# Attention begun after two token groups, gates and pools woven into its steps, pool chains cut into pieces

## What is computed

```python
z = h @ w_in[i]                                   # (B,S,3072)
q, k, v, g_attn, u, g_pool = ...                  # six slices of 512 columns each
lam = exp(sum(lam_q1*lam_k1)) - exp(sum(lam_q2*lam_k2)) + lam_init
# 4 heads, each with two 64-wide halves of q and k, and a 128-wide v; causal
o = (softmax(q1 k1^T / 8) - lam * softmax(q2 k2^T / 8)) v
attn_out = rms_norm(o, subln_g) * (1 - lam_init) * silu(g_attn)
# group g of 4: trailing mean over 2, 4, 8, 16 tokens, minus the token, then a 128x128 map
pool_out = ((mean_w(u) - u) @ w_pool) * pool_scale * silu(g_pool)
mix = concat([attn_out, pool_out]) @ w_out
h = layer_norm(2**0.25 * h + mix, ln_g, ln_b)
h = h + (p @ w_pe) * sigmoid(h @ w_pg + b_pg)
```

## Time and profile before

| | |
|---|---|
| device time, median of 3 (range) | 635.16 us (634.19 to 635.40) |
| profiled execution: device time, span | 635.05 us, 633.5 us |
| PE matmul busy | 598.1 us, 94% of the span |
| DVE busy | 383.1 us, 60% |
| ACT busy | 358.2 us, 57% |
| POOL busy | 158.5 us, 25% |
| mean granted PE clock, cores | 0.985 to 0.993 |

### The profile page before, as it was taken

The page is one execution under the profiler, slowest core; times in us unless marked ns, Lnnn a source line. Parts: engine busy times, 40 slices in busy tenths (PEclk is TensorE's granted clock), DMA queues, the critical chain, the costliest instruction groups (busy, mean ns, idle before and its releaser), DMA issues.

```text
span 633.5 us, 12632 instructions; the slowest of 8 cores (627.6 to 633.5 us)
## 1 busy us (share of the span) xinstructions
PE 598.1 (94%) x5282; PEld 331.5 (52%) x5282; DVE 383.1 (60%) x735; ACT 358.2 (57%) x520; POOL 158.5 (25%) x212
## 2 busy tenths in 40 slices
PE   6897999999999999999999999899999999999895
PEld 2343444446566554566666654455655566665442
DVE  2226833725767788344534664677876686687696
ACT  3210231348777774677788756376666566776132
POOL 0477530001111120101010110323333333333242
PEclk9999999999999999999999999899999999999899
DMA  8999904022040000401144199001211211131003
GB/s 234 319 304 298 264 9 67 0 34 34 2 68 1 2 3 1 67 1 33 37 70 67 34 134 223 10 2 67 69 67 67 68 68 67 67 135 67 34 34 133
DMA packets 28393, 51.64 MB, mean 82 GB/s; under 512 B 3248, under 2 KB 12848, under 8 KB 28336
## 3 DMA queue, kind: packets, MB, share of 16 engines
q1 hardware_dynamic: 18656, 40.61, 20.3%
q0 software_dynamic: 9680, 10.22, 10.8%
HBM read 52.66 MB, written 8.39 MB: 96 GB/s over the span
## 4 chain that ended last, share of the span: by engine, by line
PE 76%; DVE 10%; SPq 5%; DMA 3%; issue 2%; ACT 2%; POOL 1%; DVEq 0%; ACTq 0%
PE psum_all L541 29%; PE psum_all L852 17%; PE psum_all L819 10%; PE psum_all L682 8%; PE psum_all L749 7%; SPq L154 5%; PE psum_all L775 2%; DMA sb_kT<-w_in 2%; DVE sb_PT L835 1%; DMA sb_kT<-xT 1%; PE psum_all L727 1%; DVE sb_st L687 1%; DVE sb_arena L608 1%; ACT sb_PT L825 1%; POOL sb_mv L693 1%
## 5 line engine op out<-in xcount | busy, mean ns | idle before, releaser
L825 ACT ACTIVATE sb_PT<-psum_all 128x1024 bf16<-128x1024 f32 (+1 forms) x288 | 265.3, 973 | 113.0 <-PE psum_all L819 111.8
L541 PE MATMUL psum_all<-sb_xb,sb_wsec 128*128 128x512 bf16 x640 | 164.5, 386 | 11.2 <-ACT sb_wsec L429 5.2
L852 PE MATMUL psum_all<-sb_Vt,sb_PT 128*128 128x129 bf16 x2176 | 148.0, 221 | 4.6 <-DVE sb_PT L835 3.7
L852 PEld LDWEIGHTS psum_all<-sb_Vt,sb_PT 128*128 128x128 bf16 x2176 | 134.5, 98 | 33.6 <-DVE sb_PT L835 5.9
L541 PEld LDWEIGHTS psum_all<-sb_xb,sb_wsec 128*128 128x128 bf16 x640 | 57.1, 99 | 79.5 <-issue 18.9
L541 PE MATMUL psum_all<-sb_wsec,sb_xb 128*128 128x512 bf16 x384 | 94.2, 380 | 2.9 <-DVE sb_arena L596 1.3
L819 PE MATMUL psum_all<-sb_qT,sb_kT 64*128 64x256 bf16 (+1 forms) x1152 | 87.0, 267 | 1.9 <-DVE sb_mixT L633 1.5
L819 PEld LDWEIGHTS psum_all<-sb_qT,sb_kT 64*128 64x128 bf16 x1152 | 44.5, 94 | 67.0 <-ACT sb_PT L825 30.3
L682 PE MATMUL psum_all<-sb_wsec,sb_mixT 128*128 128x512 bf16 x256 | 64.0, 386 | 0.4 <-DVE sb_mixT L905 0.4
L749 PE MATMUL psum_all<-sb_wsec,sb_arena 128*128 128x512 bf16 x224 | 57.1, 384 | 4.1 <-DVE sb_arena L737 2.5
L886 POOL TENSOR_TENSOR sb_sm<-sb_sm,sb_sc 128x2 f32<-128x2 f32 x32 | 7.6, 239 | 211.8 <-ACT sb_qT L884 116.8
(11 more groups left out here) (137 smaller groups left out, 583.4 us busy)
## 6 DMA issues: line engine op xcount, KB each, us to landing
sb_Vt<-w_in SPq DMA_DIRECT2D x28, 256.0 KB, 9.9
sb_kT<-w_in SPq DMA_DIRECT2D x20, 256.0 KB, 10.0
sb_Vt<-xT SPq DMA_DIRECT2D x16, 256.0 KB, 12.3
sb_kT<-xT SPq DMA_DIRECT2D x16, 256.0 KB, 12.0
sb_xb<-xT POOLq DMA_DIRECT2D x4, 1024.0 KB, 9.9
sb_xb<-x_own SPq DMA_DIRECT2D x7, 512.0 KB, 3.5
out<-sb_xb SPq DMA_DIRECT2D x7, 512.0 KB, 2.6
sb_wsec<-w_out POOLq DMA_DIRECT2D x2, 1024.0 KB, 10.4
```

The lines of the kernel that those rows point to most:

```text
L541: P.op(PE, lambda e: e.matmul(ps[:, bank, :], a, b, start=(kc == 0), stop=(kc == 7)), reads=[B_w[sec], wk[kc], bx, xk[kc]], writes=[B_bank ...
L825: P.op(ACT, lambda e, u=u, pi=pi, q0=q0: e.activation(out=PT[pi][:, :, :, q0:256].rearrange("p k c n -> p c k n"), in_=ps[:, 2 * u:2 * u + ...
L852: P.op(PE, lambda e, u=u, k=k, s=s, kb=kb, qb=qb, c=c, pi=pi, fresh=fresh, done=done: e.matmul(ps[:, BO + qb, c * 130:c * 130 + 129], PT[p ...
```

## The change

Attention starts when groups 0 and 1 are done (k, v, and q, gate and pool of group 1). The steps of j = 1 no longer alternate with those of j = 0. There are four fills in place of three: `fill0` under j = 0 (k2, v2, k3, v3, q3), `fill1` under j = 1 and `fill2` under j = 2 (`woven` for groups 3 and 5, then k, v, q of the next own group), and `fill3` under j = 3 (gates and pool of group 7, then the output part of 13 tiles; tile 13's first product goes behind the last step). Both blocks are gone. SiLU becomes a tanh on ACT and a multiplication on DVE that both read the bank (`twice_silu`), with the factor one half moved into two constants. Pool chains go out in pieces, two at each tick (two ticks to a step); a chain still pending is flushed at the next `q_u` or `q_y`. `take` goes on behind a finished quantum when 0.6 us or more of its share is left. Temporaries move to parts of `mixT` and `qT`, and the order of the first loads changes: w_in's q columns come before the third x group, small constants before the halo.

```diff
         while t < us and self._open():
             d, done = self._one()
             t += d
-            if done:
+            if done and us - t < 0.6:
                 break
...
+        for kc in range(8):
+            round_(POOL, wsec[0][:, kc, :], fetch(w_src(0, kc)), B_wk[0][kc])
...
         def more_loads():
-            for kc in range(8):
-                round_(POOL, xb[0][:, kc, :], fetch(x_src(2, kc)), B_xk[0][kc])
+            for dst, srcd in ((hl[:], hl_d), (gscb[:], sublng_d.rearrange("d o -> o d").partition_broadcast(128)),
+                              (lamv[:], lamv_d.partition_broadcast(128))):
+                P.dma(SP, dst, srcd, dsc)
+            P.dma(SP, cnt[:], cnt_d, dsc3)
+            P.dma(SP, pscale[:], pscale_d, dsc3)
+            P.dma(POOL, tri3[:].rearrange("p c n -> p (c n)"), tri_d, dsc2)
+            P.dma(POOL, ident[:], ident_d, dsc2)
+            P.dma(POOL, wpool[:], wpool_d.rearrange("(g c) d -> c g d", c=128), dsm)
...
+            for s_ in (4, 3, 5):
+                for kc in range(8):
+                    round_(POOL, wsec[s_][:, kc, :], fetch(w_src(s_, kc)), B_wk[s_][kc])
...
         def tick():
             now[0] += 1
+            for _ in range(min(2, len(chain))):
+                chain.popleft()()
             for f in ticks.pop(now[0], []):
                 f()
...
+        def twice_silu(bank, i, out_ap, view, writes):
+            src = ps[:, bank, :].rearrange("p (a n) -> p a n", a=2)
+            P.op(ACT, lambda e: e.activation(out=gt[i][:], in_=src, func=AF.Tanh, scale=0.5), reads=[B_bank[bank]], writes=[B_gt[i]])
+            P.op(DVE, lambda e: e.scalar_tensor_tensor(out=out_ap, in0=view(gt[i][:]), scalar=1.0, in1=view(src), op0=ALU.add, op1=ALU.mult),
+                 reads=[B_gt[i], B_bank[bank]], writes=writes)
...
+            chain.extend(parts + [difference])
...
-            order += [(0, 0, h), (1, 1, h), (0, 1, h), (1, 0, h)]
-        order += [(j, hf, h) for j in (2, 3) for hf in range(2) for h in range(4)]
+            order += [(0, 0, h), (0, 1, h)]
+        order += [(j, hf, h) for j in (1, 2, 3) for hf in range(2) for h in range(4)]
...
+        side_by_side(q_v(1), range(4, 8))
+        lam_ops()
+        side_by_side(q_q(1), range(4))
+        a, o, u, g, y = parts_of(1)
+        run_all(o + u[:2] + [a[0], u[2], a[1], a[2], u[3], a[3], g[0], g[1], y[0], g[2], y[1], g[3], y[2], hook(y[3], third_own)],
+                [4, 5, 6, 7, 0, 1, 2, 3])
...
+        def woven(s, k, v, f):
+            a, o, u, g, y = parts_of(s)
+            return [a[0], k[0], a[1], k[1], a[2], k[2], a[3], k[3]] + o + [u[0], v[0], u[1], g[0], u[2], g[1], y[0], u[3],
+                                                                         g[2], y[1], g[3], y[2], hook(y[3], f)] + v[1:]
+
+        fill0 = q_k(2) + hooked(q_v(2), lambda: load_xb(4)) + q_k(3) + q_v(3) + q_q(3)
+        fill1 = woven(3, q_k(4), hooked(q_v(4), lambda: load_xb(6)), lambda: load_xb(5)) + q_k(5) + q_v(5) + q_q(5)
+        fill2 = woven(5, q_k(6), hooked(q_v(6), load_p), lambda: load_xb(7)) + q_k(7) + hooked(q_v(7), load_wout) + q_q(7)
...
+        own7 = o + [a[0], u[0], a[1], u[1], a[2], u[2], hook(a[3], out_1), hook(u[3], load_wpg)]
+        own7 += [g[0], g[1], y[0], g[2], y[1], hook(g[3], out_2), y[2], hook(y[3], out_3)]
+        fill3 = own7 + fillD
...
-        for f in both_halves(q_G, 15, 1, 0):
+        for f, f2 in zip(both_halves(q_G, 15, 1, 0), p15):
             f()
-        for f in p15:
-            f()
+            f2()
```

More of the change, by code:

```diff
@@ L369, in build_nc @@
         B_PT = [Buf() for _ in range(4)]
-        B_g = B_PT[0:2]
+        B_gt, B_psc = [Buf() for _ in range(6)], Buf()
         B_o12 = [Buf() for _ in range(6)]
-        B_rr = [Buf() for _ in range(6)]
         B_sm = [Buf() for _ in range(6)]
@@ L591, in q_halo, with go_on @@
             return [Quantum([mm(p, kc) for p in range(4) for kc in range(8)], end, 32 * 0.03)]
+        def go_on(n):
+            for _ in range(min(n, len(chain))):
+                chain.popleft()()
         def pool_chain(p, j, bank):
+            go_on(9)
             w = POOL_W[p]
@@ L990, in build_nc, with out_1, out_2, out_3 @@
                 fillD += [q_T(k)]
-        def block(s):
-            ga, gp, y = q_ga(s), q_gp(s), q_y(s)
-            run_all(ga + [gp[0], gp[1], y[0], gp[2], y[1], gp[3], y[2], y[3]], [6, 7, 0, 1, 2, 3])
-            P.op(ACT, lambda e: e.activation(out=sc[:, 8:9], in_=sc[:, 0:1], func=AF.Exp), reads=[B_sc], writes=[B_sc])
-        def start_out():
+        def out_1():
+            olds = list(B_w[3].w.values()) + list(B_w[3].r.values())
+            wload(wpe[:], wpe_d.rearrange("(kc p) n -> p kc n", p=128), [B_w[3]])
+            after(8, lambda: P.op(DVE, lambda e: e.tensor_scalar(out=wpe[:], in0=wpe[:], scalar1=0.5, scalar2=None, op0=ALU.mult),
+                                  reads=[B_w[3]], writes=[B_w[3]]))
+            P.dma(SP, lngb[:].rearrange("p a n -> p (a n)"), lng_d.partition_broadcast(128), dsv, deps=olds)
+        def out_2():
+            olds = list(B_w[5].w.values()) + list(B_w[5].r.values())
+            for dst, srcd in ((lnbb, lnb_d), (bpgb, bpg_d)):
+                P.dma(SP, dst[:].rearrange("p a n -> p (a n)"), srcd.partition_broadcast(128), dsv, deps=olds)
+            t_vec.append((dsv.sem, dsv.cnt))
+        def out_3():
             for i in (1, 2):
@@ L1092, in build_nc @@
         last = steps[NS - 1]
-        M = {(t, nh): q_M(t, nh) for t in (14, 15) for nh in range(2)}
+        M = {(t, nh): q_M(t, nh) for t in (13, 14, 15) for nh in range(2)}
         av(NS - 1)
-        finish_one()
+        feed.drain()
         for p in sorted(fins):
@@ L1102, in build_nc @@
         tail[0] = True
+        for b in B_z15:
+            inherit(b, [B_gz[3]])
         norm, q_last = q_end(last)
@@ L1105, in build_nc @@
         run("fin_o", "fin_a")
-        for q, b in rest:
-            q.end(b)
-        rest.clear()
-        stats_of(("st", 13, 0))
-        finish_one()
-        assert not feed._open()
-        for q, b in rest:
-            q.end(b)
+        pe(M[13, 0], 6)
+        pe(M[13, 1], 7)
+        M[13, 0].end(6)
+        run(("st", 13, 0))
+        M[13, 1].end(7)
+        run(("st", 13, 1), ("ag", 13))
         run("mix")
-        stats_of(("st", 13, 1), ("ag", 13))
         pe(M[14, 0], 1, 0, 7)
```

191 lines of the change are left out of this document (78 added, 113 removed).

## The result

The changed kernel takes 677.0 us (median of 4 runs, 673.94 to 679.37), the kernel before beside it 634.67 us: a ratio of 1.0656 (95% interval 1.0621 to 1.0691; the two medians alone give 1.0667), some 42 us slower. Forecast were 638.0 us and a range of 628 to 648 us. In what follows one thousandth of a ratio is 0.64 us, and every ratio is to the kernel before as it ran beside. A gain quoted between two variants is the difference of two such ratios, and its own uncertainty is 1.5 to 3 us. Runs in which the cores of a die showed a lower clock (0.81 against 0.99 in one of them) and took longer are left out of all ratios.

The account below looks back on a forecast made before the run. PE, 94% busy, was taken to set the time, so the sum was one of waits: 633.5 - 10.9 + 13.8 = 636.4 us of span, measured as 638.0 us, 0.4% slower; range 628 to 648 us.

Parts of the forecast that it names:

- item 5: First loads: small loads ahead of the halo make its weights later, adding 2.0 us (0 to 5.0).
- item 1: Steps of j = 0 and 1: pool chains in pieces remove 4.1 us of 5.1 us of waits.
- rival B: Woven lists: masks held behind `twice_silu` lengthen PE's waits until the clock falls; 650 us (643 to 652), chance 0.12.
- Items 1 and 2: Waits that go: 4.1 us in the steps of j = 0 and 1, 3.2 us at the two blocks.
- item 7: Woven lists: gates and pools on two banks make PE wait nine times, adding 9.8 us (2 to 17).
- Item 3: End of the steps: shorter wait for the last masks and less lost clock, saving 2.5 us (0 to 3.8).
- Item 4: Last instructions: one DVE pair moves ahead of the last tanh, saving 1.1 us (0.5 to 1.4).
- Item 6: DVE between about 55 and 80 us: chains, gates and maps delay the first `qk`, adding 1.0 us (0 to 3).
- Item 8: Steps of j = 3: less time to empty banks at `q_P` and `q_M`, adding 1.0 us (-2 to +6).

Follow-up runs that it names:

- experiment 3: Planner's old rule put back up to the last group: changed kernel 1.0425, with small loads and copies also moved 1.0261; new rule in the kernel before: 1.0006.

## Why the prediction was wrong, by its steps

The sign was right; the size was off by 39 us of time. Three steps failed, each shown by a run that takes it back: the planner's rule, which had no term (14.7 us alone); item 5, small loads at 2.0 us within 0 to 5.0 (9.8 us for SP's five); and item 1, where only 1.0 us of waits was left in the steps (8.4 us for the place of the transposes' copy). Together they gave back 25.1 us. The sum also had no term for a lower clock in the stretches that changed (only rival B and the bound of item 5 name one), and PE's matmuls took 13.2 us more.

- **Items 1 and 2.** Right in what goes: no wait on masks or blocks is left. Wrong in what comes there. I wrote that 1.0 us of waits would be left in j = 0 and 1, to which item 7 adds 3.4 us in j = 1; the stretch of 95 to 262 us had 13.4 us of idle time. I had priced a mask's path and not the copy of the transposes, which stands behind the masks.
- **Left out altogether:** the planner's rule, the first line of the diff. It is worth 14.7 us alone. Item 7 says: "Mostly a plain product of 1.73 us with `qk` or `av` lies between, and that hides it". That cover was made by the old rule: the rows of experiment 3 show it.
- **Item 3.** Right: the last `av` no longer waits. But an `av` at 459.83 us now waits 2.55 us for L908.
- **Item 4.** Right: 1.1 us (0.5 to 1.4) forecast, 1.5 us measured alone (0.8 to 2.2).
- **Item 5.** The failed step with its own row. The last rounding did come at "about 62" (62.55 us), and yet the cost was not 2.0 us. The two positions are not equal: in the earlier trace rows the wait at 60.29 us belongs to the section behind halo, u0 and u1; now 62.55 us is the halo's own last chunk, with all of the own group's work behind it. The halo's weights were 12 us late. I priced the issue times and not what they do to the loads behind them. SP's five loads cost 9.8 us, by run.
- **Item 6.** Taken as 1.0 us. My own list there gave DVE 7.9 + 10 + 9 = 27 us of work in a stretch of 25 us, so it could not fit. PE waited 5.52 + 1.24 us and 0.65 us more for it. The work itself also ran slower beside POOL's roundings than my rows (last section).
- **Item 7.** In kind and nearly in size right: 4.9 us in j = 1 (3.4 forecast), 4.1 in j = 2 (3.7), 2.0 in j = 3 (2.7), so 11.0 against 9.8, and 2.4 us more at the first attention gate of j = 2. They are twelve waits of 0.3 to 1.6 us and not nine, and four of them are for the map's end, L668.
- **Item 8.** 1.0 us forecast. Found: 3.7 us at P for L800, which the old kernel had not, and 2.5 us at L888. The 2.33 us of them at 606.35 us had the lower clock behind them. The wait at the first G stayed (2.5 us), as forecast.
- **The rivals.** B came nearest in its effect: waits about as long as that of the earlier trace rows or longer, with the lower clock behind them, at 55.93, 93.00, 129.84, 146.65 and 459.83 us; behind the one of 2.40 us at 273.76 us six matmuls took 1.47 us, so 2.4 GHz. The length of the wait does not decide it alone: the clock also fell behind one of 1.49 us (last section). But its mechanism (masks behind `twice_silu`) was not the one; in j = 0 there are no such gates.

What is still open: the version with all repairs and the first group's Silu is at 1.018 to 1.020, some 12 us over the old kernel. Its trace has 9.6 us of waits behind gates and maps (3.1 us of time went with one reader of the bank less), 3.7 us at P, and the first scores at 82.68 us. No run separates the rest.
